# NSA scores as three fp32r products of high and low parts, with the causal mask pass behind them

## What is computed

```python
s_s = jnp.einsum('bghqd,bgqnsd->bghqns', qp, kg).astype(jnp.float32) * scale
s_s = jnp.where(m_s[:, :, None], s_s, NEG).reshape(B, G, h, Q_BLOCK, n_top * SEL_BLOCK)
p_s = jax.nn.softmax(s_s, axis=-1).reshape(B, G, h, Q_BLOCK, n_top, SEL_BLOCK)
...
s_w = jnp.einsum('bghqd,bgkd->bghqk', qp, kwb).astype(jnp.float32) * scale
p_w = jax.nn.softmax(jnp.where(m_w, s_w, NEG), axis=-1)
...
return g[..., 0:1] * o_c + g[..., 1:2] * o_s + g[..., 2:3] * o_w
```

## Time and profile before

| what | value |
| --- | --- |
| three runs | median 2131.74 us (2131.24 to 2137.3) |
| profiled execution | 2136.14 us |
| its span | 2134.3 us, 26976 instructions |
| TensorE products, busy | 2090.1 us, 98% |
| TensorE weight loads, busy | 1659.0 us, 78% |
| VectorE, busy | 1412.9 us, 66% |
| ScalarE, busy | 928.5 us, 44% |
| GpSimd, busy | 58.5 us, 3% |
| line 288, high x high, 1856 products | 750.0 us |
| HBM | 85 GB/s over the span |

### The profile page before, as it was taken

How to read it: one execution, slowest core, us unless ns; L and a number is a source line. 1 busy time by engine, 2 the same in 40 slices (tenths; PEclk the granted TensorE clock), 3 DMA queues, 4 the chain that set the end, 5 groups by cost and what they waited for, 6 DMA issues and landing times.

```text
span 2134.3 us, 26976 instructions
## 1 busy us (share of the span) xinstructions
PE 2090.1 (98%) x10308; PEld 1659.0 (78%) x10308; DVE 1412.9 (66%) x2073; ACT 928.5 (44%) x1562; POOL 58.5 (3%) x132
## 2 busy tenths in 40 slices
PE   9999999999999999998999999999999999999998
PEld 6887777888888877776778888787777777777786
DVE  7788888777775355565677776447667648465664
ACT  5576765344443244444454443224344222444531
POOL 0000001000000001111000000000000000000000
PEclk9999999999999999999999999999999999999999
DMA  4321222232222342110233323332222224111132
GB/s 167 122 77 60 70 70 70 89 98 91 97 98 83 93 132 77 50 60 30 69 99 99 98 91 94 87 107 88 72 72 76 71 68 158 50 50 49 46 103 80
DMA packets 55074, 179.47 MB, mean 84 GB/s; under 512 B 6159, under 2 KB 7311, under 8 KB 54840
## 3 DMA queue, kind: packets, MB, share of 16 engines
q1 hardware_dynamic: 51264, 167.79, 24.6%
q10 hardware_dynamic: 3704, 10.30, 1.4%
HBM read 175.95 MB, written 4.74 MB: 85 GB/s over the span
## 4 chain that ended last, share of the span: by engine, by line
PE 81%; DVE 3%; ACT 1%; issue 1%; DMA 0%; POOL 0%; DVEq 0%; ACTq 0%
PE bankpair L288 23%; PE bankpair L292 23%; PE bankpair L289 22%; PE bankpair L1471 1%; PE bankpair L722 1%; PE bankpair L1503 1%; PE bankpair L1484 1%; PE bankpair L742 1%; PE bankpair L1317 1%; PE bankpair L1329 1%; PE bankpair L732 1%; PE bankpair L687 1%; PE bankpair L1331 0%; PE bankpair L1450 0%; PE bankpair L1415 0%
## 5 line engine op out<-in xcount | busy, mean ns | idle before, releaser
L288 PE MATMUL bankpair<-scaled_in_high,weights_high 128*128 128x512 f32 x1856 | 750.0, 404 | 7.7 <-DVE padded_rows L2381 3.1
L289 PE MATMUL bankpair<-scaled_in_low,weights_high 128*128 128x512 f32 x1856 | 727.6, 392 | 0.0
L312 ACT ACTIVATE weights_high<-weight_ring 128x1024 fp32r<-128x1024 f32 (+3 forms) x344 | 333.9, 972 | 309.3 <-DMA weight_ring<-down_dram 155.7
L292 PE MATMUL bankpair<-scaled_in_high,weights_low 128*128 128x512 f32 x1856 | 465.1, 389 | 0.0
L288 PEld LDWEIGHTS bankpair<-scaled_in_high,weights_high 128*128 128x128 f32 x1856 | 351.0, 189 | 94.3 <-issue 6.9
L323 DVE TENSOR_TENSOR weights_low<-weight_ring,weights_high 128x1024 fp32r<-128x1024 f32 (+3 forms) x344 | 383.8, 1125 | 55.5 <-ACT weights_high L312 46.0
L289 PEld LDWEIGHTS bankpair<-scaled_in_low,weights_high 128*128 128x128 f32 x1856 | 351.1, 189 | 76.2 <-issue 5.7
L292 PEld LDWEIGHTS bankpair<-scaled_in_high,weights_low 128*128 128x128 f32 x1856 | 348.5, 188 | 73.0
L288 PE MATMUL bankpair<-gated_high,weights_high 128*128 128x512 f32 x448 | 178.1, 397 | 0.7 <-DVE gated_high L1970 0.7
L289 PE MATMUL bankpair<-gated_low,weights_high 128*128 128x512 f32 x384 | 151.9, 395 | 0.0
L585 DVE SCALAR_TENSOR_TENSOR conv_rows<-padded_rows,params,conv_rows 128x512 f32<-128x512 f32 x176 | 131.8, 749 | 7.0 <-ACT conv_rows L554 3.8
(11 more groups left out here) (373 smaller groups left out, 2408.6 us busy)
## 6 DMA issues: line engine op xcount, KB each, us to landing
weight_ring<-up_dram SPq DMA_DIRECT2D x88, 512.0 KB, 3.6
weight_ring<-w_in_dram SPq DMA_DIRECT2D x70, 512.0 KB, 3.6
weight_ring<-in_w_dram SPq DMA_DIRECT2D x40, 512.0 KB, 3.7
weight_ring<-down_dram SPq DMA_DIRECT2D x32, 384.0 KB, 3.1
weight_ring<-kvq_dram SPq DMA_DIRECT2D x24, 512.0 KB, 3.6
weight_ring<-down_dram SPq DMA_DIRECT2D x32, 320.0 KB, 2.9
weight_ring<-out_a_dram SPq DMA_DIRECT2D x8, 512.0 KB, 3.8
weight_ring<-out_b_dram SPq DMA_DIRECT2D x8, 512.0 KB, 3.7
```

The costliest lines, as they stand in the source:

```text
L288: nc.tensor.matmul(bank, WH[:, high_slot, cell], high, start=(k == 0), stop=False)
L289: nc.tensor.matmul(bank, WH[:, high_slot, cell], low, start=False, stop=False)
L292: mm = nc.tensor.matmul(bank, WL[:, slot, cell], high, start=False, stop=(c == last_k))
L312: nc.scalar.activation(WH[:, (PART0[name] + k) % SLOTS, 0:n], RAW[:, b % SLOTS, 0:n], ACT.Copy).then_inc(high_ready, 1)
```

## The change

The rotated queries and keys are split in a high and a low part, as other inputs of the kernel are. ScalarE copies each of the six tiles to fp32r (`rope_high`), VectorE subtracts that from the tile (`rope_low`). The low part takes the place of its own tile; the high parts go to places in the arena that are free at that time, seen through a new fp32r name of the arena (`ROUNDED`). `KS`, `QR` of head pair 0 and `KW` (`PARTS_ORDER`) are split ahead of the loop; the tiles of head pairs 1, 2 and 3 in steps 5, 10 and 18 on ScalarE and 6, 12 and 20 on VectorE. The scores become three fp32r products for each group, each over all (i + 1) x 128 keys at once: high x high, low x high, high x low. The mask's product is added to the diagonal block behind them. `nsa_scores` waits for the parts that it reads. Two gate rows that lay in two tiles of the arena's end (`SGB[0]`, `SGB[1]`) now lie in `padded_rows`.

```diff
+        with ExitStack() as rounded_arena:
+            ROUNDED = rounded_arena.enter_context(nc.sbuf_tensor("rounded_arena", [P, AREA], F32R))
...
-        SGB = [sec(T), sec(T), KVC[:, 0, :], KVC[:, 1, :], SQ[:, 0, :], SQ[:, 1, :], ACC[:, :], STD[:, :]]
+        SGB = [U[:, 0, 0:T], U[:, 1, 0:T], KVC[:, 0, :], KVC[:, 1, :], SQ[:, 0, :], SQ[:, 1, :], ACC[:, :], STD[:, :]]
...
+        ROPED = [QR[:, x, :] for x in range(NP_)] + [KS, KW]
+        ROPE_LOW = [ROUNDED[:, at:at + T] for at in [qr_at + x * T for x in range(NP_)] + [ks_at, ks_at + T]]
+        ROPE_HIGH = [ROUNDED[:, at:at + T] for at in (cw_at + 7 * T, yn_at + 3 * T, qr_at, qr_at + T, cos_at, cos_at + T)]
+        PARTS_ORDER = (NP_, 0, NP_ + 1, 1, 2, 3)
...
                 n = (i + 1) * P
-                pe.wait_ge(roped, 6)
                 if w >= 1:
                     pe.wait_ge(n_p, 2 * w)
-                for g in range(2):
-                    nc.tensor.matmul(BANK[2 + g][:, i * P:n], ONEHOT[:, :], FUTURE[:, :], start=True, stop=False)
-                for at in (slice(i * P, n), slice(0, i * P))[0:1 + (i > 0)]:
+                pe.wait_ge(roped, 6 + max(3 + j, 2 + c if j == 0 else 0))
+                x, y = j, NP_ + c
+                for t, (q, k) in enumerate(((ROPE_HIGH, ROPE_HIGH), (ROPE_LOW, ROPE_HIGH), (ROPE_HIGH, ROPE_LOW))):
                     for g in range(2):
                         half = slice(64 * g, 64 * g + 64)
-                        mm = nc.tensor.matmul(BANK[2 + g][:, at], QR[half, j, i * P:n], (KS, KW)[c][half, at],
-                                              start=at.start < i * P, stop=True)
+                        nc.tensor.matmul(BANK[2 + g][:, 0:n], q[x][half, i * P:n], k[y][half, 0:n], start=(t == 0), stop=False)
+                for g in range(2):
+                    mm = nc.tensor.matmul(BANK[2 + g][:, i * P:n], ONEHOT[:, :], FUTURE[:, :], start=False, stop=True)
                 mm.then_inc(n_s, 1)
...
+            def rope_high(n):
+                act.wait_ge(roped, 6)
+                x = PARTS_ORDER[n]
+                nc.scalar.activation(ROPE_HIGH[x], ROPED[x], ACT.Copy).then_inc(rope_act, 1)
+
+            for n in range(3):
+                rope_high(n)
             cmp_exp(0)
             cmp_turned(0)
             for w in range(NSA_STEPS + 2):
+                if w in (5, 10, 18):
+                    rope_high((5, 10, 18).index(w) + 3)
...
+            def rope_low(n):
+                dve.wait_ge(rope_act, 3 + n + 1)
+                x = PARTS_ORDER[n]
+                ro.step(nc.vector.tensor_tensor(ROPE_LOW[x], ROPED[x], ROPE_HIGH[x].bitcast(F32), ALU.subtract))
+
+            for n in range(3):
+                rope_low(n)
             cmp_logits(0)
             cmp_probs(0)
             for w in range(NSA_STEPS + 2):
...
                     maxima(w)
+                if w in (6, 12, 20):
+                    rope_low((6, 12, 20).index(w) + 3)
```

More of the change, by code:

```diff
@@ L1154, in three_parts @@
         YA = sec(2 * MH, T)
+        yn_at = sec.at
         YN = sec(NP_, T)
@@ L1174, in three_parts @@
         KVC = sec(2, T)
+        ks_at = sec.at
         KS, KW = sec(T), sec(T)
         VS, VW = sec(NT, P), sec(NT, P)
+        qr_at = sec.at
         QR = sec(NP_, T)
```

## The result

The changed kernel took 2136.48 us (median of 11 executions, 2134.11 to 2139.8), the kernel before 2131.31 (11 executions, 2130.27 to 2137.3). The ratio is 1.0020, 95% interval 1.0011 to 1.0029: 4.3 us slower (2.3 to 6.2), under the 0.3% (6.4 us) that was set as the bound of no change. The forecast was 2132.4, 0.7 us more than before. Sign and range held; the size did not, by a factor of six.

The account below looks back on a forecast made before the run. TensorE, busy 98% of the span, was taken as the bound. Terms -0.1 - 0.15 + 1.0 = +0.7 us put the 2131.74 median at 2132.4; the range took in 2129.5 and reached up to 2139.

Parts of the forecast that it names:

- Score products and mask: TensorE, 32 loop steps: fp32r scores with the mask behind them change step times by +0.15, -0.01, -0.05, -0.10; -0.1 us.
- the first rival: Score steps on TensorE: pairs of fp32r products do not overlap, +14.9 us, in all 2147.3; chance 0.13.
- fast loads: Score products on TensorE: fp32r weights load as fast as bf16, -2.7 us, 2129.7; chance 0.10.
- a slow rate for short products: Score products on TensorE: a 128-column fp32r product takes as long as a whole float32 one, +2.9 us; chance 0.07.
- The splits of the later head pairs: ScalarE copies and VectorE subtractions in steps 5/6, 10/12 and 18/20: hidden behind existing waits, 0 us.
- The first three splits: Ahead of the loop: VectorE's three subtractions delay the compressed probabilities, so TensorE waits at step 0's transposes; +1.0 us.
- the upper bound that the prediction named: Splits ahead of the loop: all of the three subtractions' time shows up as loss, 2.1 us.
- The clock rival: Thin stretch 1835.7 to 1838.7 us: the granted clock falls once more, +1.7 us, 2134.1; chance 0.22.
- a granted clock under 1 after 1835 us: Sign of being wrong: the clock is granted below full after 1835 us, around step 0; no size given.
- the signs for the products: Score steps in the timeline: scores to mask 0.48, 0.54, 0.71, 0.88 us; dense products to scores 0.32.

Follow-up runs that it names:

- before_with_stall: The kernel before, plus three unread 128x512 subtractions on VectorE ahead of the first compressed logits; 2137.45 us, ratio 1.0022.
- early_splits: The changed kernel with the first three splits moved earlier, where VectorE was idle; 2132.05 us, ratio 1.0002 to the kernel before.
- early_splits_stall_in_loop: early_splits plus seven unread 128x512 subtractions on VectorE ahead of the probabilities in step 23; 2135.59 us, ratio 1.0007.
- products_by_group: early_splits with the three score products of group 0 issued ahead of the three of group 1; 2134.77 us, ratio 0.9998.

## Why the prediction was right, and where it was not

- *Score products and mask, -0.1 us.* Held. The four sizes came out at +0.15, 0, -0.04 and -0.09, +0.2 in all by eight steps of each, and the loop behind the scores of step 1 is 0.3 us shorter. Pairs of fp32r products overlap, so the first rival is excluded. Short products run at the weight loads' pace: an fp32r load lasts 187 ns in its record, like the float32 one,

```profile
L1479 PEld LDWEIGHTS bankpair<-rounded_arena 64*128 64x128 f32 x186 | 14.1, 187 | 11.6 <-issue 11.2
```

and three pairs of 128 columns take 0.48, so neither fast loads nor a slow rate for short products shows here. The added change of shape costs its 0.09. The Trainium skill (TensorEngine Tiling, key properties) says that changing the tiling mode drains TensorE, and the trace agrees, with the 0.09.
- *The splits of the later head pairs, 0.* Held: no new wait in the loop.
- *The first three splits, +1.0 us.* This is the term that was mis-sized. Its mechanism was right to the instruction (VectorE's three subtractions, the late probabilities, TensorE's wait at the transposes) and its size was not. The 1.0 was measured against TensorE's arrival in the profile of before, where the half clock of 1830 to 1835 had made TensorE 1.7 us late. That lateness hid over half of the wait. In an execution without that fall the same work leaves 2.4 us of waiting: the upper bound that the prediction named, 2.1, with the 0.2 to 0.3 that are waited for even without the splits.
- *The clock rival, chance 0.22, +1.7.* This is what came on top, as `before_with_stall` shows by itself, and it too was undersized: the rival had 3.4 us more at half clock (1.7 us of time), the profiles have 6.8 more than that of before, and 10.2 more than that of `early_splits`, which cost 3.9 us. Wait and clock should not have been priced apart. The wait is longest where TensorE arrives at full clock, and in all four profiles with a wait of 1.8 us or more the clock fell behind it.
- *The signs.* Of the signs of being wrong that it named, a granted clock under 1 after 1835 us came true (0.50 until 1842); the signs for the products came out within 0.02 us.
- *The range.* It held partly by luck. Its upper end took in a slow rate of short products (+2.9), which does not exist here, and the scatter of the runs; forecast and clock rival together reach only 2134.1.
- *Slips in the working.* In the first rival three pitches double, not five, as its own +0.33 has it. For fast weight loads the terms given add up to 2.5, not 2.7, and two places have 2129.7 and 2129.5 for one time. Neither moves the forecast.
- *The sum against one execution.* The kernel's clock differs from execution to execution ahead of the change, so a single profile fixes neither TensorE's lateness nor what the clock does next. A term that depends on it should have been priced at both clocks.

## What to carry to other kernels

Work that is put ahead of a chain on a side engine costs what the chain then makes the bound engine wait, and the slack has to be taken for an execution in which the bound engine arrives early, at full clock. Where the bound engine's own work is thin around that place, count the clock too: the wait of 2.4 us there came with 10.2 us of half clock, and two waits of 1.63 and 0.77 us amid dense products with none. Three passes in place of a whole float32 product gain little when blocks are short, because each pass brings a weight load of its own (0.11 us per pair here), and each change of tile shape costs 0.09 us.

## What the runs showed of the hardware that was not expected

- A program's time up to one point differs between executions by nearly 5 us with the same instructions (1824.2 and 1829.1 us), and the kernel before scattered from 2130.3 to 2137.3. The granted clock accounts for both: 5.0 us in the windows of the two profiles, and 6.4 us from 0.992 to 0.989 over the executions.
- Behind a stretch of narrow products with a wait of 1.8 to 2.5 us in it the clock stayed at half for 6.8 and 10.2 us, while dense products were already running again; around two waits of 1.63 and 0.77 us amid dense products it did not fall. It fell for 3.4 us near step 0 also in three profiles (of the kernel before, `early_splits_stall_in_loop` and `products_by_group`) with 0.2 us of waiting for the probabilities or none. With 4.6 us of waiting it fell later, 1838, and for 6.8 us only.
- Two halves of the array work side by side on products that were issued one half after the other: 0.91 and 0.90 us for the six products in the two orders.
- What remains open: whether the clock's fall at step 0 sets in with a certain wait or only becomes more frequent with it. The mean granted clock of each execution says how much was at half clock in all, not where.
